# Expert inputs as 512 latents a chunk and one prompt product for four chunks, with late chunks split by ScalarE and VectorE

## The reference

```python
def block(xb):
    q = (xb @ wq).reshape(tb, PEER_HEADS, 2, PEER_DK // 2)
    sc = jnp.einsum('thsd,hskd->thsk', q, subkeys)
    sv, si = lax.top_k(sc, PEER_TOPK)
    cand = sv[:, :, 0, :, None] + sv[:, :, 1, None, :]      # 256 candidates per head
    best, ci = lax.top_k(cand, PEER_TOPK)
    idx = i1 * N_KEYS + i2                                  # 128 experts per token
    gsm = jax.nn.softmax(best, axis=-1)
    act = jax.nn.gelu(jnp.einsum('td,thkd->thk', xb, u_tab[idx]))
    return jnp.einsum('thk,thkd->td', gsm * act, v_tab[idx])
```

## Time and profile before

| | |
|---|---|
| median of 3 runs | 4620.28 us (4614.63 to 4627.97) |
| profiled execution | 4617.94 us, its span 4616.1 us |
| mean granted TensorE clock | 0.976 |
| TensorE matmul busy | 4415.5 us, 96% |
| VectorE busy | 3265.7 us, 71% |
| ScalarE busy | 1197.8 us, 26% |
| GpSimd busy | 1945.9 us, 42% |
| DMA | 797.70 MB, mean 173 GB/s |

### The profile page before, as it was taken

How to read it: one execution, slowest core, us unless ns; L and a number is a source line. 1 busy time by engine, 2 the same in 40 slices (tenths; PEclk the granted TensorE clock), 3 DMA queues, 4 the chain that set the end, 5 groups by cost and what they waited for, 6 DMA issues and landing times.

```text
span 4616.1 us, 76065 instructions
## 1 busy us (share of the span) xinstructions
PE 4415.5 (96%) x27516; PEld 4019.7 (87%) x27516; DVE 3265.7 (71%) x6397; ACT 1197.8 (26%) x1696; POOL 1945.9 (42%) x1206
## 2 busy tenths in 40 slices
PE   7878999999999999999988889999999999999998
PEld 6857999999999988888886689999999999888887
DVE  6873199969999597877633432993599995766665
ACT  2043110022332233333233420101232332333332
POOL 2322455644444364444341134555444443544440
PEclk9978999999999999999998999999999999999999
DMA  5401234548777898888520012444477778888884
GB/s 202 161 19 46 67 112 125 181 118 165 161 153 159 218 354 312 312 314 309 204 74 23 24 60 67 119 125 118 117 159 163 158 152 241 321 287 294 288 287 141
DMA packets 823654, 797.70 MB, mean 173 GB/s; under 512 B 566513, under 2 KB 601041, under 8 KB 822898
## 3 DMA queue, kind: packets, MB, share of 16 engines
q1 hardware_dynamic: 175248, 500.38, 32.6%
q10 hardware_dynamic: 603106, 159.70, 16.1%
q0 software_dynamic: 45056, 134.38, 8.3%
HBM read 640.41 MB, written 153.89 MB: 172 GB/s over the span
## 4 chain that ended last, share of the span: by engine, by line
PE 82%; ACTq 8%; DVE 5%; ACT 3%; issue 2%; DMA 0%; DVEq 0%
PE acc L515 14%; PE acc L517 14%; PE acc L516 14%; PE aux L758 5%; PE acc L760 5%; PE acc L758 5%; PE aux L760 5%; PE aux L759 5%; PE acc L759 5%; ACTq L1048 4%; ACTq L1081 4%; PE aux L730 2%; PE aux L573 1%; ACT gates L1098 1%; PE aux L680 1%
## 5 line engine op out<-in xcount | busy, mean ns | idle before, releaser
L515 PE MATMUL acc<-a_hi,w_hi 128*128 128x320 f32 x5296 | 1673.5, 316 | 45.8 <-DVE a_lo L1288 32.9
L517 PE MATMUL acc<-a_hi,w_lo 128*128 128x320 f32 x5296 | 1643.8, 310 | 0.1
L516 PE MATMUL acc<-a_lo,w_hi 128*128 128x320 f32 x5296 | 1643.5, 310 | 0.0
L515 PEld LDWEIGHTS acc<-a_hi,w_hi 128*128 128x128 f32 x5296 | 1000.6, 189 | 50.9 <-issue 34.5
L516 PEld LDWEIGHTS acc<-a_lo,w_hi 128*128 128x128 f32 x5296 | 1000.9, 189 | 1.7 <-issue 0.5
L517 PEld LDWEIGHTS acc<-a_hi,w_lo 128*128 128x128 f32 x5296 | 999.0, 189 | 0.5 <-issue 0.3
L442 POOL TENSOR_TENSOR w_lo<-w_in,w_hi 128x1024 fp32r<-128x1024 f32 (+1 forms) x345 | 902.4, 2616 | 27.6
L458 POOL CAST w_hi<-w_in 128x1024 fp32r<-128x1024 f32 x256 | 311.3, 1216 | 1041.7 <-DMA w_in<-in_u 1041.7
L1526 DVE SCALAR_TENSOR_TENSOR one_b<-iota_b,picks_t 128x384 bf16<-128x384 bf16 x1024 | 632.9, 618 | 0.0
L1524 DVE TENSOR_SCALAR one_a<-iota_b,picks_t 128x128 bf16<-128x128 bf16 x1024 | 573.1, 560 | 60.0 <-PE aux L730 55.0
L467 POOL DMA_INDIRECT found<-in_v,where_i x256 | 315.3, 1231 | 509.1 <-DVE total L1586 401.7
(11 more groups left out here) (246 smaller groups left out, 5423.1 us busy)
## 6 DMA issues: line engine op xcount, KB each, us to landing
w_in<-in_u SPq DMA_DIRECT2D x256, 512.0 KB, 4.0
w_in<-in_v SPq DMA_DIRECT2D x256, 512.0 KB, 4.8
gate_s<-gates ACTq DMA_DIRECT2D x64, 1024.0 KB, 14.0
ag<-act_s SPq DMA_DIRECT2D x256, 256.0 KB, 5.0
ag<-gate_s SPq DMA_DIRECT2D x256, 256.0 KB, 6.1
act_s<-a_out ACTq DMA_DIRECT2D x184, 256.0 KB, 3.7
act_s<-tmp ACTq DMA_DIRECT2D x72, 256.0 KB, 3.6
w_in<-in_in SPq DMA_DIRECT2D x32, 512.0 KB, 4.6
```

Source lines behind the costliest of these rows:

```text
L515: pe.matmul(out, wh, hi[:, k, n], start=(k == 0), stop=False)
L516: pe.matmul(out, wh, lo[:, k, n], start=False, stop=False)
L517: return pe.matmul(out, wl, hi[:, k, n], start=False, stop=(k == kt - 1))
```

## The change

- The chunk of inputs is computed for the 512 latents alone, 24 matmuls of 512 columns into one bank of `acc[0]` (`latent_steps`). After four chunks, one product for the prompt follows, 24 matmuls in which 128 tokens of `a_hi`, `a_lo` stand still and four chunks' weights are streamed, into a bank of `acc[1]` (`prompt_steps`).
- `act_p` is laid out with a token's experts side by side; it is stored once per four chunks (`prompt` on ScalarE), and the index of a pick is formed accordingly, and earlier on VectorE.
- SyncE loads a chunk when the prompt product that used its slot is done, so that four slots come free together. The slots are numbered so that each layer's chunk 0 of kind "u" lies in slot 0.
- 60 chunks run ahead of the gates, 64 beside them, 4 behind. The two gate groups beside a chunk come after its fourth and eighth step.
- GpSimd splits chunks 0 to 63 (`LATE`); ScalarE (`high_u`) and VectorE (`low_u`) split chunks 64 to 127.
- At the start of the value stage, the order of loads and splits follows the new slots.

```diff
-        BRIDGE = 1
-        BUILT = 2
+        BRIDGE = GROUP
+        LATE = NKEY // 2
...
             if kind == "v":
                 return v_done, NKEY * layer + i + 1
+            if kind == "u":
+                return made_p, NKEY // GROUP * layer + i // GROUP + 1
...
+                def load_inputs(i, u):
+                    if isinstance(i, int) and i == 0:
+                        sp.wait_ge(*last_use(BEFORE[UC[l] + u]))
+                    else:
+                        sp.wait_ge(made_p, FOURS * l + u // GROUP - 1 + 2 * i)
+                    sp.dma_start(landing(u), a["u"][l, bass.ds(u + SPLIT * i, 1)].rearrange("o p n -> (o p) n"))\
+                      .then_inc(raw_in[u], 16)
...
+                def latent_steps(m0, w, taken_value, split, split_value):
+
+                    pe.wait_ge(split, split_value)
+                    pe.wait_ge(taken[m0 % 2], taken_value)
+                    for k in range(KD):
+                        mm = linear_step(acc[0][:, m0 % 2, :], w, P, k, KD, a_hi, a_lo, slice(P, T))
+                        if k == KD - 1:
+                            mm.then_inc(made, 1)
+                        yield
+
+                def prompt_steps(g, first_slot, bank):
+
+                    if l or not (isinstance(g, int) and g < 2):
+                        pe.wait_ge(taken_p, FOURS * l + g - 1)
+                    w, n = slice(first_slot, first_slot + GROUP), slice(0, P)
+                    for k in range(KD):
+                        wh, wl = w_hi[:, w, k * P:(k + 1) * P], w_lo[:, w, k * P:(k + 1) * P]
+                        pe.matmul(acc[1][:, bank, :], a_hi[:, k, n], wh, start=(k == 0), stop=False)
+                        pe.matmul(acc[1][:, bank, :], a_lo[:, k, n], wh, start=False, stop=False)
+                        mm = pe.matmul(acc[1][:, bank, :], a_hi[:, k, n], wl, start=False, stop=(k == KD - 1))
+                        if k == KD - 1:
+                            mm.then_inc(made_p, 1)
+                        yield
...
+                def prompt(g, k):
+
+                    act.wait_ge(made_p, FOURS * l + g + 1)
+                    if not (isinstance(g, int) and g < 2 and l == 0):
+                        act.wait_ge(p_st[k], 16 * (FOURS // 2) * l + 8 * (g - k))
+                    act.activation(p_out[k][:], acc[1][:, k, :], ACT.Gelu_apprx_tanh).then_inc(taken_p, 1)
+                    act.wait_ge(taken_p, FOURS * l + g + 1)
+                    act.dma_start(act_p_rows[l][:, bass.ds(4 * P * g, 4 * P)], p_out[k][:]).then_inc(p_st[k], 16)
...
+                        for j in range(GROUP):
+                            take_gates(i, g, 2 * j)
+                            take_chunk(j)
+                            if j == GROUP - 1:
+                                high_u(first + GROUP + 2, i)
+                                high_u(first + GROUP + 3, i)
+                            take_gates(i, g, 2 * j + 1)
+                            if j in (1, 2):
+                                high_u(first + GROUP + j - 1, i)
+                        prompt(first // GROUP + 4 * i, first // GROUP % 2)
...
                         ins.then_inc(hot_ready, 1)
+                        for j in ((), (0,), (1,), (2, 3))[max(0, q % 8 - 4)]:
+                            low_u(LATE + GROUP * (q // 8) + j, i)
+
+                def low_u(c, i):
+
+                    dve.wait_ge(hi_v, input_by_both(l, c) + 4 * GROUP * i)
+                    dve.tensor_tensor(w_lo[:, c % SPLIT, :], landing(c % SPLIT), w_hi[:, c % SPLIT, :].bitcast(F),
+                                      ALU.subtract).then_inc(lo_v, 1)
```

More of the change, by code:

```diff
@@ L49, with slots @@
 CHUNKS, PRODUCTS = plan()
+def slots():
+    slot, before, loads, had = [], [], [], {}
+    start = {l: next(n for n, c in enumerate(CHUNKS) if c[:2] == (l, "u")) for l in range(2)}
+    for n, chunk in enumerate(CHUNKS):
+        w = (n - start[chunk[0]]) % SPLIT
+        last, count = had.get(w, (None, 0))
+        slot.append(w)
+        before.append(last)
+        loads.append(count + 1)
+        had[w] = n, count + 1
+    return slot, before, loads
+SLOT, BEFORE, LOADS = slots()
 def chunk_at(layer, kind):
@@ L97, in build @@
         iota_b = sb("iota_b", [P, P], BF)
+        mask_at = end[0]
         mask = sb("mask", [P, 384])
@@ L265, in build @@
         OCTETS = PICKS // 8
+        FOURS = NKEY // GROUP
         GROUPS = NL_TOK // GROUP
@@ new lines, in four_chunks @@
+                def four_chunks(c, i, far, split, split_value, between=None):
+                    done = 0
+                    for j in range(GROUP + 1):
+                        if j < GROUP:
+                            m0 = UM[l] + c + j
+                            steps = latent_steps(m0, (c + j) % SPLIT, m0 // 2 + far // 2 * i, split,
+                                                 split_value(c + j) + far * i)
+                        else:
+                            steps = prompt_steps(c // GROUP + far // GROUP * i, c % SPLIT, c // GROUP % 2)
+                        for _ in steps:
+                            done += 1
+                            if between is not None and done % 4 == 0 and j < GROUP:
+                                between(done // 4 - 1)
@@ new lines, in by_pool, with by_both, early @@
+                def by_pool(c):
+                    return split_by_pool(UC[l] + c)
+                def by_both(c):
+                    return input_by_both(l, c)
+                def early(i):
+                    for c in (0, GROUP):
+                        four_chunks(c, i, SPLIT, lo_done, by_pool)
+                for m in (UM[l] - 2, UM[l] - 1):
+                    has_taken(pe, m)
+                early(0)
+                with pe.Fori(1, EARLY) as i:
+                    early(i)
+                four_chunks(EARLY * SPLIT, 0, 0, lo_done, by_pool)
@@ L774, in values @@
                                     has_taken(pe, m)
+                            if first and u == 0 and dt == 6:
+                                pe.wait_ge(taken_p, FOURS * (l + 1))
                             mm = value_step(dt, u, first and u == 0, False)
@@ L808, in _ @@
             pe.wait_ge(v_taken, 16)
-            first = chunk_at(1, "dzv") % SPLIT
+            first = SLOT[chunk_at(1, "dzv")]
             for i, tiles in enumerate(((0, 1), (2, 3), (4,))):
```

224 lines of the change are left out of this document (107 added, 117 removed).

## The result

| | before | after |
|---|---|---|
| median of the runs | 4621.48 us, 4 runs (4614.63 to 4627.97) | 4769.03 us, 4 runs (4761.82 to 4781.15) |
| profiled execution | 4617.94 | 4771.22 |
| mean granted TensorE clock | 0.976 | 0.958 |
| ratio | | 1.0327, 95% interval 1.0301 to 1.0354 |

Two single executions, 6261.35 us of experiment 2's kernel and 8418.48 us of experiment 7's, belong to a slow state and are left out of what follows.

What follows compares the result with a forecast made beforehand. TensorE was taken to bound the kernel, with ScalarE's shut queue deciding the late chunks. Per layer -15.4 + 29 + 4 - 2 = +15.6, two layers +31, +2 once: 4651 profiled, 4653 us median, range 4578 to 4710.

Steps and rivals of the forecast that it cites:

- What bounds the kernel: Whole kernel before: TensorE, 96% busy, sets the time; ScalarE's DMA issues, 4% each at two lines, are the exceptions.
- Part 1: Input chunks without gates: four take 27.2 us by measured matmul spacing, saving 15.4 us a layer.
- Part 2: Late chunks' splits on ScalarE and VectorE: VectorE has time enough, about 0.9 us wait at the eighth gate group, falling into slack.
- Part 3: Late chunks beside gates: ScalarE's order sets the pace, 36.7 us for four against 34.9, +29 us a layer.
- 19.3 + W: Late input stage: predicted time in us for four chunks, with the third latents waiting for ScalarE to free a bank.
- W: Stretch from the first gate store until ScalarE's queue opens: 16.2 us before, 17.4 forecast, bounds 15.8 to 19.5.
- the tail: Four chunks without gates after each layer's last gates: a wait of about 5 us against about 1, +4 a layer.
- Part 4: Ends of the stages: +4 a layer after the last gates, -2 at the first gate group, +2 once between layers.
- The sum: Whole kernel: +15.6 us a layer, +33 in all on the profiled execution, 4651, or 4653 as median.
- Rival 2: Late chunks: input loads fully serial with the gate stores, 38.8 us for four, +51 a layer, 4724 us; chance 0.13.
- Rival 3: Late chunks: ScalarE not held because the prompt's store is small, 33.5 us for four, 4542 us; chance 0.06.

Runs made afterwards that it cites:

- experiment 2: Changed kernel with SyncE's loads spread: the first of four slots after the prompt product, the others beside the next group's latents; 4647.87 us, ratio 1.0055.
- experiment 7: Changed kernel with SyncE instead of ScalarE issuing the gate stores, between one group's loads and the next; 4561.66 us, ratio 0.9867.
- experiment 4: Changed kernel with GpSimd splitting all 128 chunks, without ScalarE's late conversions and VectorE's late subtractions; 4812.07 us, ratio 1.0411.
- the filler: Changed kernel with 18 unread matmuls of 512 columns on TensorE before the third latents of each late group; 4722.66 us, ratio 1.0220.

## Why the prediction was wrong, by its own steps

**What bounds the kernel** held: TensorE, and ScalarE's shut queue as the exception that matters.

**Part 1** held to the digit: 27.2 us for four early chunks. The spacing measured elsewhere in the trace carried over.

**Part 2** held: one_a's median is 0.25 us with no long ones in the late stage, one-hots make TensorE wait 6.8 us in 15 pieces of at most 0.7 (0.9 was forecast), and experiment 4 prices the move at 43 us.

**Part 3** had ScalarE's order and the formula 19.3 + W right. The step that failed is its size, in two places: "I take 17.4" for W, and no term for TensorE's clock.
- W measured 19.1 (18.0 to 20.3), the stated upper end of 19.5 nearly reached. The error was in where the value between the bounds was put: at the dearest stretch of before (17.3), though four loads were coming. That is 1.7 us of each four chunks. The bounds themselves came out well by luck: the prediction read the 16.2 of the earlier trace rows as a stretch with one load and the 17.3 as one with two, and made 1.1 us a load of the difference. SyncE issues a second load within the stretch in both, at 13.05 us in the earlier trace rows and at 10.7 in the earlier trace rows, and stretches with like loads run from 15.2 to 17.3. The difference was scatter, and the measured price per load happens to be 1.1 too.
- The formula had no term for TensorE's clock. It forecast a wait of 2.8 us at each third latents (W less the 14.6 that it gives as the point where the wait begins), and priced what comes after at full speed. The wait was 4.5, and the matmuls behind it ran at 0.50: 1.6 us by the filler. The profile of before could have warned: the gate group behind the 5.3 us wait of the earlier trace rows starts at 999.44, and the windows view gives 0.50 there (columns as above).

```profile
999.20:1002.40 3.20, 2.96 (x18) 2.96 (x19) 3.20 (x11) 0.00 (x0) 0.00 (x0) 0.50 0.00 0
```


Of the 3.9 us by which four late chunks (40.6, mean of both layers) exceed the forecast 36.7, W has 1.7 and the clock 1.6. The last 0.6 isn't explained; it is mostly layer 1's, where the pace with filler is still 1.0 over the formula. The prediction's own sum with W at 19.1 gives 4710, the upper end of its range (38.4 for four, 6.4 - 1 for the tail, +44 a layer): it is the missing clock, in the main, that took the time outside.

**Part 4** was small and mostly right. TensorE's wait for one-hots at the first gates of layer 0 is 3.2 us where it was 5.3, the forecast's -2. Chunks 123 to 127 take 36.3 and 36.0 us, 9 over the 27.2 of four without gates, where 5 were forecast: W and the clock again. The change of layers cost nothing where +2 was forecast: from the gelu of layer 0's chunk 127 to that of layer 1's chunk 0 the traces have 1273.2 us before and 1278.5 after, and 5.4 of these are the last prompt product.

**The sum** counted one stretch too many: there are 16 in a layer, and the last of them is the tail's, so that 15 late groups, not 16, have the wait. Per layer the miss is then 15 x 3.9 for the pace, -3.6 for the one group at 33.1 instead of 36.7, and +4 for the tail: 59. Two layers make 118, and the profiled execution, 4771.2, lies 120 over the 4651.

**The rivals.** Rival 2 (fully serial loads) was the true one for W, and with a chance of 0.13 it was given too little. Its 4724 is, by chance, what the filler gives: its mechanism with the clock put right. Rival 3 had the right number for the wrong kernel: with ScalarE really not held, 4542 was forecast (4544 with the 2.3 us by which the other sums go over to the median) and 4554 to 4562 measured.

## What to carry to other kernels

When a step makes transfers come together that came one by one, look whether another engine's large store of small pieces is in flight then, and take the high end for how long that engine's queue stays shut. A wait of several microseconds on TensorE is to be priced with the slow matmuls behind it, here 1.6 us on top of 4.5. Put a DMA of many small pieces on the queue of an engine for which nobody waits within its length, and look what stands behind it there: the same edit made one version 4.3% faster and the other 1.5% slower.

## What the runs showed of the hardware that I had not expected

- Four loads of 512 KB issued on SyncE from 2.6 us after ScalarE's first gate store lengthen the pair of stores from 7.5 to 10.6 us and W from 15.8 to 19.1 (means). With two of them in the first 10 us, W is 16.7. When the four come from 3.9 us on (experiment 4), the pair keeps its 7.4 us and W is still 19.3.
- Two 1 MB stores of 128-byte pieces shut the queue of their own issuer: while ScalarE's issue stands, SyncE issues four loads in 3.40 us (2.15 us at 644.17, with no gate stores out), and while SyncE's stands, ScalarE issues in 0.34 us.
- Eighteen useless matmuls per group, 4.34 us, make the kernel 46 us faster, since the matmuls behind the hole, some nine in the mean, no longer run at 0.50.
